# The second feed-forward product of a two-layer decoder trunk as seven half-size products per chunk

## What is computed

```python
def _sqrelu_mlp(h, w1, w2):
    return jnp.square(jax.nn.relu(h @ w1)) @ w2

for i in range(DEPTH):                      # DEPTH = 2
    x = x + mixer_i(_rmsnorm(x, norm_i))    # 0: _fox_attention, 1: _dilated_attention
    x = x + _sqrelu_mlp(_rmsnorm(x, mlp_norm[i]), mlp_w1[i], mlp_w2[i])
```

## Time and profile before

| | before |
|---|---|
| median of 3 runs | 1649.92 us (1649.57 to 1650.88) |
| the profiled execution | 1646.14 us, span 1644.4 us |
| mean granted TensorE clock | 0.997 |
| busy: PE, DVE, ACT, POOL | 1598.6, 816.6, 599.7, 355.9 us |
| chain that ended last | PE 84%, of it 74% the matmuls of L467; DVE 5%, POOL 4% |
| DMA | 139.93 MB, mean 85 GB/s |

### The profile page before, as it was taken

The page is one execution under the profiler, slowest core; times in us unless marked ns, Lnnn a source line. Parts: engine busy times, 40 slices in busy tenths (PEclk is TensorE's granted clock), DMA queues, the critical chain, the costliest instruction groups (busy, mean ns, idle before and its releaser), DMA issues.

```text
span 1644.4 us, 23363 instructions
## 1 busy us (share of the span) xinstructions
PE 1598.6 (97%) x8858; PEld 1329.6 (81%) x8866; DVE 816.6 (50%) x1468; ACT 599.7 (36%) x1068; POOL 355.9 (22%) x534
## 2 busy tenths in 40 slices
PE   7999988999999999999999999999989999999999
PEld 6776655888888888899988889998767888888887
DVE  4456566444444444444647576546564443434342
ACT  5433333432323233434434443434442432323230
POOL 3412100050000000263528364535621000000000
PEclk9999999999999999999999999999999999999999
DMA  6211110223232323332222412222223232323232
GB/s 170 83 59 40 54 38 14 90 90 107 85 112 80 115 77 104 127 90 78 65 77 77 129 54 78 65 78 65 86 71 116 77 106 86 110 82 103 88 101 79
DMA packets 77562, 139.93 MB, mean 85 GB/s; under 512 B 12192, under 2 KB 12192, under 8 KB 77216
## 3 DMA queue, kind: packets, MB, share of 16 engines
q1 hardware_dynamic: 75280, 134.51, 26.9%
q10 hardware_dynamic: 2192, 4.20, 0.7%
HBM read 132.33 MB, written 6.36 MB: 84 GB/s over the span
## 4 chain that ended last, share of the span: by engine, by line
PE 84%; DVE 5%; POOL 4%; issue 2%; ACT 2%; SPq 1%; DMA 0%; ACTq 0%; POOLq 0%; DVEq 0%
PE ps L467 74%; PE ps L525 3%; PE ps L555 2%; POOL qrs L1332 2%; PE ps L567 2%; PE ps L539 2%; DVE pT_sb L1112 1%; POOL qss L1331 1%; PE ps L498 1%; ACT w_h L786 1%; DVE qss L1023 1%; ACT sq L824 1%; ACT p_sb L850 1%; PE ps L519 1%; DVE ps L1056 0%
## 5 line engine op out<-in xcount | busy, mean ns | idle before, releaser
L467 PE MATMUL ps<-w_h,act_h 128*128 128x512 f32 x768 | 317.1, 413 | 5.4 <-DVE w_l L997 3.4
L467 PE MATMUL ps<-w_h,act_l 128*128 128x512 f32 x768 | 307.0, 400 | 0.0
L467 PE MATMUL ps<-w_l,act_h 128*128 128x512 f32 x768 | 305.8, 398 | 0.0
L786 ACT ACTIVATE w_h<-w_raw,gain_t 128x512 fp32r<-128x512 f32 x316 | 209.8, 717 | 148.3 <-PE ps L467 102.4
L997 DVE SCALAR_TENSOR_TENSOR w_l<-w_raw,gain_t,w_h 128x512 fp32r<-128x512 f32 x316 | 226.8, 759 | 59.1 <-ACT w_h L786 59.0
L467 PE MATMUL ps<-w_h,hid_h 128*128 128x512 f32 x640 | 252.7, 395 | 0.1
L467 PE MATMUL ps<-w_l,hid_h 128*128 128x512 f32 x640 | 250.1, 391 | 0.0
L467 PE MATMUL ps<-w_h,hid_l 128*128 128x512 f32 x640 | 249.5, 390 | 0.0
L467 PEld LDWEIGHTS ps<-w_h,act_h 128*128 128x128 f32 x768 | 192.0, 250 | 24.3 <-issue 7.9
L467 PEld LDWEIGHTS ps<-w_l,act_h 128*128 128x128 f32 x768 | 192.1, 250 | 16.0
L467 PEld LDWEIGHTS ps<-w_h,act_l 128*128 128x128 f32 x768 | 193.0, 251 | 14.4
(11 more groups left out here) (150 smaller groups left out, 1847.5 us busy)
## 6 DMA issues: line engine op xcount, KB each, us to landing
w_raw<-in_mlp_w SPq DMA_DIRECT2D x128, 512.0 KB, 3.7
w_raw<-in_dil_w_in SPq DMA_DIRECT2D x72, 512.0 KB, 3.7
w_raw<-in_fox_w_in SPq DMA_DIRECT2D x22, 512.0 KB, 3.6
w_raw<-in_fox_w_out SPq DMA_DIRECT2D x8, 512.0 KB, 3.8
w_raw<-in_dil_w_out SPq DMA_DIRECT2D x8, 512.0 KB, 3.8
acc_kept<-acc SPq DMA_DIRECT2D x2, 1056.0 KB, 6.6
o_sb<-acc_kept SPq DMA_DIRECT2D x2, 1056.0 KB, 5.2
x_sb<-in_x SPq DMA_DIRECT2D x4, 512.0 KB, 8.5
```

Source lines behind the costliest of these rows:

```text
L467: return mm(ps_out, lhs[i], rhs[j], start=(k == 0 and term == 0), stop=(k == KT - 1 and term == 2))
L786: last = fn(w_h[:, u % WR, j, :], raw(u)[:, j, :], ACT.Copy, scale=gain_t[:, norm, k:k + 1])
```

## The change

The second product of a chunk, A x B with A the squared hidden units (512 tokens x 1024) and B the weights (1024 x 1024), is cut into halves in each direction and computed by Winograd's form of Strassen's scheme, from seven products of half size instead of eight: A11xB11, S1xT1, S2xT2, A12xB21, S3xT3, S4xB22 and A22xT4. Each has 2 banks (256 tokens x 512 columns) over a depth of 4 blocks.

- The sums S1 = A21 + A22, S2 = S1 - A11, S3 = A11 - A21 and S4 = A12 - S2 are made by DVE behind the squares (`sums`), block by block; T1 = B12 - B11, T2 = B22 - T1, T3 = B22 - B12 and T4 = B21 - T2 by GpSimd on the raw weights (`combine`), 1024 columns at a time.
- The low halves of A11, S1 and S2 are made by DVE block by block (`a11_low`, `s12_low`); those of A12, S3, S4 and A22 by GpSimd in one operation each (`lazy_low`), once their slot of `op_h` is free.
- Products that go into more than one part of the result are added over all chunks into four running sums in SBUF (`e_all`), which GpSimd clears before the stage and DVE folds into x in the last chunk (`finish`). DVE waits for the clearing (`sums_clear`) before the first square of the stage. The other three go straight to x.
- Weights are loaded in 8 raw slots; the split weights have a ring of three pairs. The gain of the norm is no longer in the first weights: DVE multiplies it into the turned x in `prepare`.

```diff
+A11_B11, S1_T1, S2_T2, A12_B21, S3_T3, S4_B22, A22_T4 = range(PRODUCTS)
+OPERAND_SLOT = [0, 1, 2, 0, 1, 2, 0]
+ADDS_TO = {A12_B21: (0, 1), S3_T3: (1, 0), S4_B22: (0, 0), A22_T4: (1, 1)}
+SUMS = [A11_B11, S1_T1, S2_T2, S3_T3]
+LAZY = [A12_B21, S3_T3, S4_B22, A22_T4]
...
+def w_slot(p):
+    return 2 * [0, 1, 0, 1, 2, 0, 1, 2, 0, 1, 2][p // 2] + p % 2
+def w_slot_free(p):
+    return [-4, -2, 2, 4, 0, 6, 8, 10, 12, 14, 16][p // 2]
...
+        mlp_raw = [w_raw[:, 0, :, :], w_raw[:, 1, :, :], p_sb[:, :, :], pT_sb[:, :, :]] + [raw4[:, j, :, :] for j in range(4)]
+        SLOT_B12, SLOT_B22, SLOT_B11, SLOT_B21 = 0, 2, 4, 6
+        mlp_ps = [(ps_s[0], ps_s[1]), (ps_q, ps_o), (ps_proj[0], ps_proj[1])]
...
+                def seventh(i, q, tau):
+                    if q == A11_B11 and tau == 0:
+                        pe.wait_ge(x_added, i * ADDS + x0)
+                    elif q == S2_T2:
+                        pe.wait_ge(sqr_done, i * 8 + (8 * c0 + 7 + tau))
+                    elif q >= 3:
+                        pe.wait_ge(x_added, i * ADDS + (x0 + 2 * (q - 3) + tau + 1))
+                    o, ps_out = OPERAND_SLOT[q], mlp_ps[q % 3][tau]
+                    for k in range(KH):
+                        p = 8 + 2 * q + k // 2
+                        if tau == 0:
+                            if k % 2 == 0:
+                                pe.wait_ge(wl_done, mlp_unit(layer, i, p) + 1)
+                            if q == A11_B11:
+                                pe.wait_ge(opl_done, i * 8 + (8 * c0 + 2 * k + 1))
+                            elif q == S1_T1:
+                                pe.wait_ge(opl_done, i * 8 + (8 * c0 + 2 * k + 2))
+                            elif q in LAZY and k == 0:
+                                pe.wait_ge(lazyl_done, i * 4 + (4 * c0 + LAZY.index(q) + 1))
+                        lhs = [x[:, o, k, tau * P:(tau + 1) * P] for x in (op_h, op_l)]
+                        rhs = [x[w_slot(p)][:, k % 2, :] for x in (w_h, w_l)]
+                        for term in range(3):
+                            a, b = [(0, 0), (1, 0), (0, 1)][term]
+                            last = mm(ps_out[:, :], lhs[a], rhs[b], start=k == 0 and term == 0, stop=k == KH - 1 and term == 2)
+                    last.then_inc(proj_full, 1)
...
+                    for b in range(KT):
+                        for k in range(KT // 2 if b == 0 else 0, KT):
+                            hidden(i, b, k)
+                    for q in range(PRODUCTS):
+                        seventh(i, q, 0)
+                        if final and layer == 0 and q == A22_T4:
+                            prepare(3, 0, 0)
+                            prepare(3, 0, 1)
+                        seventh(i, q, 1)
+                        if final and layer == 0 and q in (S3_T3, S4_B22):
+                            for t, half in PREP_AFTER_MLP[2 * (q - S3_T3):2 * (q - S3_T3) + 2]:
+                                prepare(3, half, t)
...
+                def lazy_high(i, q):
+                    z, o = LAZY.index(q), OPERAND_SLOT[q]
+                    act.wait_ge(s34_done, i * 4 + 4 * (c0 + 1))
+                    before = max(p for p in range(q) if OPERAND_SLOT[p] == o)
+                    act.wait_ge(proj_full, mlp_unit(layer, i, 8 + 2 * before + 2))
+                    s0 = {A12_B21: 8, A22_T4: 12, S4_B22: 16, S3_T3: 20}[q]
+                    nc.scalar.copy(op_h[:, o, :, :], hr[:, s0:s0 + 4, :]).then_inc(oph_done, 1)
...
+                src = prep_bank(n, t, half)[:, :].rearrange("p (k t) -> p k t", k=4)
+                if n in PREP_OF_MLP:
+                    dve.wait_ge(prep_full, prep_no(n, t, half) + 1)
+                    dve.wait_ge(actl_done, prep_no(n, t, half))
+                    tmp = sq[:, :].rearrange("p (k t) -> p k t", k=4)
+                    gain = gain_t[:, PREP_OF_NORM.index(n), 4 * half:4 * half + 4].unsqueeze(2).broadcast_to([P, 4, P])
+                    v.tensor_tensor(tmp, src, gain, ALU.mult).then_inc(scaled, 1)
+                    src = tmp
                 dve.wait_ge(acth_done, prep_no(n, t, half) + 1)
...
+                def square(i, b):
+                    dve.wait_ge(relu_done, i * 8 + (8 * c0 + b + 1))
+                    k = b // 2
+                    dst = hr[:, 8 + k:13 + k:4, :] if b % 2 else hr[:, 4 * (k % 2):4 * (k % 2) + 4:3, :]
+                    v.scalar_tensor_tensor(dst, ps_proj[b % 2][:, :].rearrange("p (a t) -> p a t", a=2), 0.0,
+                                           qn[:, b % 2, :].rearrange("p (a t) -> p a t", a=2), ALU.max, ALU.mult).then_inc(sqr_done, 1)
+                def sums(i, k):
+                    r = 4 * (k % 2)
+                    a11, s1, s2, a21 = (hr[:, r + j, :] for j in range(4))
+                    a12, a22, s4, s3 = (hr[:, 8 + 4 * j + k, :] for j in range(4))
+                    dve.wait_ge(sqr_done, i * 8 + (8 * c0 + 2 * k + 2))
+                    v.tensor_tensor(s1, a21, a22, ALU.add).then_inc(s12_done, 1)
+                    v.tensor_tensor(s3, a11, a21, ALU.subtract)
+                    dve.wait_ge(s12_done, i * 8 + (8 * c0 + 2 * k + 1))
+                    v.tensor_tensor(s2, s1, a11, ALU.subtract).then_inc(s12_done, 1)
+                    dve.wait_ge(s12_done, i * 8 + (8 * c0 + 2 * k + 2))
+                    v.tensor_tensor(s4, a12, s2, ALU.subtract).then_inc(s34_done, 1)
+                def a11_low(i, k):
+                    dve.wait_ge(oph_done, i * 12 + (12 * c0 + 2 * k + 1))
+                    v.tensor_tensor(op_l[:, 0, k, :], hr[:, 4 * (k % 2), :], f(op_h[:, 0, k, :]), ALU.subtract).then_inc(opl_done, 1)
+                def s12_low(i, k):
+                    dve.wait_ge(oph_done, i * 12 + (12 * c0 + 2 * k + 2))
+                    r = 4 * (k % 2)
+                    v.tensor_tensor(op_l[:, 1:3, k, :], hr[:, r + 1:r + 3, :], f(op_h[:, 1:3, k, :]), ALU.subtract).then_inc(opl_done, 1)
...
+                def add(i, q, tau, final):
+                    dve.wait_ge(proj_full, mlp_unit(layer, i, 8 + 2 * q + tau) + 1)
+                    dve.wait_ge(x_added, i * ADDS + x0)
+                    ps_in = mlp_ps[q % 3][tau][:, :]
+                    if q in SUMS:
+                        e = e_sum[SUMS.index(q)][:, tau, :]
+                        last = v.tensor_tensor(e, ps_in, e, ALU.add)
+                        if final:
+                            last = finish(q, tau, last)
+                    else:
+                        dst, scale = tile(*ADDS_TO[q][:1], tau, *ADDS_TO[q][1:])
+                        if final:
+                            dve.wait_ge(dve_own, own[0])
+                        last = v.scalar_tensor_tensor(dst, ps_in, scale, dst, ALU.mult, ALU.add)
+                    last.then_inc(x_added, 1)
+                def finish(q, tau, last):
+                    e11, e1, e22, e33 = (e[:, tau, :] for e in e_sum)
+                    def scaled(th, half, e):
+                        dst, scale = tile(th, tau, half)
+                        return v.scalar_tensor_tensor(dst, e, scale, dst, ALU.mult, ALU.add)
+                    if q == S1_T1:
+                        return last
+                    link(last)
+                    if q == A11_B11:
+                        link(scaled(0, 1, e11))
+                        return v.tensor_tensor(e22, e22, e11, ALU.add)
+                    if q == S2_T2:
+                        link(scaled(0, 0, e1))
+                        link(scaled(0, 0, e22))
+                        link(scaled(1, 0, e1))
+                        return v.tensor_tensor(e33, e33, e22, ALU.add)
+                    link(scaled(1, 1, e33))
+                    return scaled(1, 0, e33)
...
                 dve.wait_ge(xrs_done, 2 * layer + 2)
+                dve.wait_ge(sums_clear, layer + 1)
...
+            def mlp(layer):
+                c0 = CHUNKS * layer
+                def loaded(i, slot):
+                    pool.wait_ge(raw_in[slot], i * 32 + 16 * (mlp_loads(layer, slot) + 2))
+                def split(i, q, h):
+                    pool.wait_ge(wl_done, mlp_unit(layer, i, 8 + 2 * q + h) + 1)
+                def combine(dst, a, b):
+                    g.tensor_tensor(mlp_raw[dst], mlp_raw[a], mlp_raw[b], ALU.subtract).then_inc(t_done, 1)
+                def lazy_low(i, q):
+                    o, z = OPERAND_SLOT[q], LAZY.index(q)
+                    pool.wait_ge(oph_done, i * 12 + (12 * c0 + 8 + z + 1))
+                    s0 = {A12_B21: 8, A22_T4: 12, S4_B22: 16, S3_T3: 20}[q]
+                    g.tensor_tensor(op_l[:, o, :, :], hr[:, s0:s0 + 4, :], f(op_h[:, o, :, :]), ALU.subtract).then_inc(lazyl_done, 1)
+                pool.wait_ge(proj_full, BANK_MLP[layer])
+                for e in e_sum:
+                    last = g.memset(e, 0.0)
+                last.then_inc(sums_clear, 1)
+                with pool.Fori(0, CHUNKS) as i:
+                    for h in range(2):
+                        loaded(i, SLOT_B12 + h)
+                        split(i, A11_B11, h)
```

(41 more changed lines are left out.)

409 lines of the change are left out of this document (252 added, 157 removed).

## The result

| | before | after |
|---|---|---|
| median | 1649.74 us | 1721.3 us (1721.2 to 1722.65, 4 runs) |
| ratio to before | | 1.0441, 95% interval 1.0425 to 1.0457 |
| profiled execution, span | 1644.4 us | 1720.9 us |
| mean granted TensorE clock | 0.997 | 0.974 |

The change makes the kernel 4.4% slower, 76.5 us by the two spans, where 1703 us had been forecast. First the page of after: the line of busy times, which answers to the earlier trace rows, and the chain that ended last, which answers to the earlier trace rows.

What follows compares the result with a forecast made beforehand. TensorE, busy 97% of the span, was taken to bound the kernel. One bank fewer per chunk (-43.6 us) against added waits and slow clock summed to +53.3, forecast 1703 us on the 1649.9 median; range 1655 to 1728.

Steps and rivals of the forecast that it cites:

- product 0, last quarter: First product of each chunk: PE waits for the low half of the operand's last block, 1.46 x 8 = +11.7 us.
- product 4 in six chunks: GpSimd and DVE taking turns make product 4 start 3.3 us late in six chunks, +19.8 us.
- last chunk, layer 1, with its end: Folding the running sums delays weight halves in layer 1's last chunk, +14.3 us, and 0.7 at the end.
- last chunk, layer 0: Folding plus PE's transposes of x and wait for x delay products 5, 6 and the next stage, +22 us.
- the clearing, with its slow clock: Start of layer 0: first square waits for GpSimd's memsets behind the rotation tables, +22 us, plus 2.2 for slower PE.
- 1.46 x 8 = +11.7 us: Product 0 in eight chunks: nine matmuls cover 2.04 of 3.5 us until the last low half is ready.
- 5.0 + 7 x 2.1 + 6 x 1.13: Before product 4: seven GpSimd operations and six DVE weight halves, one after the other, end at 26.5 us, 3.3 late.
- the case of only POOL waiting: Product phase: only POOL is held up beside DVE; same product phase cost, cheaper last chunks, some 1688 us in all.
- I add 2.2 here and 2 for the two last chunks: Slower PE clock after gaps: 2.2 us at layer 0's start, 2 for the last chunks (bounds 0 and 8).
- The first: Feed-forward stages: GpSimd and DVE hardly meet, product phase +0, sum +3.4, 1653 us; chance 0.17.
- The faster rival: Start of layer 0: clearing not late, worth 24 us, deciding only if contention is light too; chance 0.07.
- What would show it: Signs: PE busy falls some 43 us, idle rises some 95; clearing wait about 22; weight halves some 1.8 on average.

Runs made afterwards that it cites:

- e9: Changed kernel with GpSimd's sums T and late low halves on DVE, rotation tables before the norm's factors, product 0 reordered, folding later: 1634.8 us (ratio 0.9923).
- e5: Changed kernel with PE issuing blocks 0 to 2 of both halves of product 0, then block 3 of both: 1720.7 us (ratio 1.0447).
- e3: Changed kernel with each 1024-column GpSimd subtraction of the feed-forward stage replaced by one of 8 columns and eight memsets, not computing those results: 1652.2 us (ratio 1.0029).
- e8: Changed kernel with the eight sums T and four late low halves of each chunk on DVE instead of GpSimd: 1669.0 us (ratio 1.0133).
- e4: Changed kernel with 16 extra matmuls on constant operands ahead of product 4 in the six chunks of the hardware loops: 1709.5 us (ratio 1.0372).
- e1: Changed kernel with GpSimd building rotation tables and mask ahead of the norm's factors of layer 0: 1700.4 us (ratio 1.0316).

## Why the prediction was right, and where its terms were off

Against the span of before, where the 76.5 us are. The 1.8 us are an average worked out from the spacing of the plain chunks. The last chunks are what remains of their stage (400.0 against 352.5 us in layer 0, and 21.9 us more in layer 1) when the other rows are taken off.

| term | forecast | measured |
|---|---|---|
| one bank per chunk | -43.6 | -43.6 (no gap in the plain chunks of e9) |
| product 0, last quarter | +11.7 | 1.45 x 8 = +11.6 |
| product 4 in six chunks | +19.8 | 4.15 x 6 = +24.9 |
| slow clock behind product 4's gap | 0 | 1.8 x 6 = +10.8 |
| last chunk, layer 1, with its end | +15.0 | +18.4 |
| last chunk, layer 0 | +22 | +22.7 |
| the clearing, with its slow clock | +24.2 | 19.5 + 1.8 = +21.3 |
| starts of layers; slow clock of the last chunks (measured within theirs) | +4.2 | +3.2, and 1.1 in the out-projection |
| second mixer | 0 | +6.1 |

Direction, mechanism and places were right. The forecast was 18 us low by the medians (1703 against 1721.3), and 23.2 by the two profiled executions of the table (53.3 against 76.5). Point by point:

- **"1.46 x 8 = +11.7 us"** was right to 0.01 us, as a gap. As a price it was not a term of its own: e5 took it away and gained nothing, because GpSimd's lateness stands behind it. It became worth something only without GpSimd.
- **"5.0 + 7 x 2.1 + 6 x 1.13"**: the mechanism is shown by e3 and e8, the size was a little off. In the first chunk six turns took 3.35 us each, not 3.23, and the remaining operation 2.73 (397.99 to 400.72, for the most part alone), not 2.1. That is 1.3 us more; GpSimd also began 0.3 us sooner, and the gap was 0.85 more than forecast. Over the second product DVE's halves took 2.14 us on average, not some 1.8. The Trainium skill's rule ("SBUF — State Buffer", section "SBUF: two separate sides") is borne out: both engines stand still, DVE's half rises from 1.22 to 3.38 us and GpSimd's operation from 2.40 to 3.39, and the case of only POOL waiting is out.
- **"I add 2.2 here and 2 for the two last chunks"** is the step that failed. The slow clock was seen in the earlier trace rows and charged to the long gap and to the last chunks alone. It follows each gap of about 4 us just the same, at some 1.8 us, and e4 took 10 to 12 us of it away without touching any lateness (by its plain chunks and by the medians). Matmuls at the low clock cost some 27 us in all: 11.8 in the six plain chunks, 5.1 and 4.6 in the two last ones, 1.8 behind the clearing, 1.6 at the start of layer 1 and 2.0 at the start of the second mixer (the table has what is over its six times 1.8 in layer 1's row). 4.2 had been charged, and that difference is about the whole miss; the other errors nearly cancel.
- **The last chunks** came out close partly by luck. In layer 1 the gaps ahead of products 3, 4 and 5 were 2.9, 2.9 and 4.5 us, 10.2 together, where 4.8, 1.4 and 8.1 had been forecast. The slow clock, 5.1 us there and more at the layer's start and in its second chunk, made up the difference. In layer 0 the gaps add up to 17.2 and the slow matmuls to 4.6.
- **The second mixer** was not in the sum at all. Its 6.1 us are in part the clock: 2.0 are slow matmuls behind the gap of 3.4 us that ends where it begins. The rest are small waits of PE, which rose from 13.7 to 18.0 us (21.2 with the wait in front); in e9 they are 16.1 (20.3 with the wait in front). No run takes a cause of these away, so it stays open.
- **The rivals.** The first put 1653 us on engines that hardly meet, with GpSimd's work still there; e3 has 1652.2. Its condition was false, and its sum was about right, though the closeness is partly luck: e3's steps are also shorter than GpSimd's. Turns decided the size of the loss, as was argued from four operations of the earlier trace rows, but not its sign: e3, without them, is still 0.3% above before, and only e9, with the other losses gone too, is below it. The faster rival's condition, a clearing in time, is e1: it gains its 21 us, and not the rest, which the rival also said.
- **What would show it**: POOL's shortest subtraction is 2.39 us and those in the middle 3.39, the memsets end at 357.1, long behind the square's turn, and the gaps are where they were foretold, except that no wait for weight halves in the last chunks reached 8 us (the longest gap there was 4.5; the one of 7.9 in layer 0 is a wait for x). PE's busy time was to fall by 43 us and fell by 9, since matmuls at the low clock are longer: the clock again.
